# Moving the second layer's modulation sums from the first mixer into the second and third

## The reference

```python
def second_block(x, c, ada_w, ada_b, ln_g, ln_b, ...):
    cond = jax.nn.silu(c)
    for l in range(DEPTH_2):                                   # 2 layers
        mod = (cond @ ada_w[l] + ada_b[l])[:, None, :]         # 1024 -> 6 * 1024
        sh_m, sc_m, g_m, sh_f, sc_f, g_f = jnp.split(mod, 6, axis=-1)
        h = x * (1.0 + sc_m) + sh_m
        y = even_mixer(h, ...) if l % 2 == 0 else spatial_gating_mixer(h, ...)
        x = layer_norm_2(ALPHA * x + (1.0 + g_m) * y, ln_g[l, 0], ln_b[l, 0])
        h = x * (1.0 + sc_f) + sh_f
        y = swiglu(h, ...) if l % 2 == 0 else moe_swiglu(h, ...)
        x = layer_norm_2(ALPHA * x + (1.0 + g_f) * y, ln_g[l, 1], ln_b[l, 1])
    return x
```

## Time and profile before

| what | value |
|---|---|
| three executions, median (lowest to highest) | 2375.59 us (2375.39 to 2376.65) |
| the profiled execution, its own time | 2377.7 us |
| its span in the trace | 2375.9 us |
| TensorE matmul busy | 2269.4 us (96%) |
| VectorE busy | 1608.5 us (68%) |
| ScalarE busy | 1297.5 us (55%) |
| read from HBM | 635.29 MB |
| TensorE clock granted, mean over the span | 0.982 |

### The profile page before, as it was taken

The page is one execution under the profiler, slowest core; times in us unless marked ns, Lnnn a source line. Parts: engine busy times, 40 slices in busy tenths (PEclk is TensorE's granted clock), DMA queues, the critical chain, the costliest instruction groups (busy, mean ns, idle before and its releaser), DMA issues.

```text
span 2375.9 us, 25462 instructions
## 1 busy us (share of the span) xinstructions
PE 2269.4 (96%) x10290; PEld 1857.8 (78%) x10290; DVE 1608.5 (68%) x1897; ACT 1297.5 (55%) x1562; POOL 0.4 (0%) x6
## 2 busy tenths in 40 slices
PE   8999999998999979799989899999999999999997
PEld 7668877887888866578848788888888888888886
DVE  0266233546889863345423698989898998989895
ACT  1245113105677743334320587877777787878784
POOL 0000000000000000000000000000000000000000
PEclk9999999997999999999999799999999999999999
DMA  8465455745998862045440498999999898989892
GB/s 345 185 255 213 178 212 233 274 195 223 359 356 327 325 266 107 1 177 213 161 176 1 194 391 335 365 347 354 349 353 377 325 372 327 374 328 376 326 374 96
DMA packets 51217, 638.14 MB, mean 269 GB/s; under 512 B 8737, under 2 KB 10638, under 8 KB 12302
## 3 DMA queue, kind: packets, MB, share of 16 engines
q1 hardware_dynamic: 48526, 630.33, 69.1%
q10 hardware_dynamic: 2560, 6.03, 0.7%
HBM read 635.29 MB, written 1.05 MB: 268 GB/s over the span
## 4 chain that ended last, share of the span: by engine, by line
PE 91%; DVE 4%; ACT 2%; DMA 2%; issue 1%; SPq 0%; DVEq 0%; ACTq 0%
PE psum L1697 56%; PE psum L1487 19%; PE psum L1479 5%; PE psum L1707 2%; PE psum L1581 2%; PE psum L1720 2%; PE psum L1787 2%; DMA ring<-w_in 1%; DMA ring<-w_branch_in 1%; DVE stage_lo L1338 1%; PE psum L1592 0%; ACT arena L546 0%; DMA ring<-w_in_in 0%; DVE arena L559 0%; PE psum L1509 0%
## 5 line engine op out<-in xcount | busy, mean ns | idle before, releaser
L1338 DVE TENSOR_TENSOR stage_lo<-ring,stage_hi 128x1024 fp32r<-128x1024 f32 (+1 forms) x934 | 1109.6, 1218 | 107.4 <-ACT stage_hi L926 82.7
L926 ACT ACTIVATE stage_hi<-ring 128x1024 fp32r<-128x1024 f32 (+1 forms) x934 | 965.3, 1056 | 279.0 <-PE psum L1697 247.9
L1697 PE MATMUL psum<-stage_hi,x_hi 128*128 128x512 f32 (+1 forms) x1344 | 529.1, 394 | 14.2 <-DVE x_lo L1320 11.5
L1697 PE MATMUL psum<-stage_hi,x_lo 128*128 128x512 f32 (+1 forms) x1344 | 522.3, 389 | 0.0
L1697 PE MATMUL psum<-stage_lo,x_hi 128*128 128x512 f32 (+1 forms) x1344 | 521.1, 388 | 0.0
L1697 PEld LDWEIGHTS psum<-stage_hi,x_hi 128*128 128x128 f32 x1344 | 253.2, 188 | 64.1 <-issue 11.9
L1697 PEld LDWEIGHTS psum<-stage_hi,x_lo 128*128 128x128 f32 x1344 | 253.0, 188 | 53.0
L1697 PEld LDWEIGHTS psum<-stage_lo,x_hi 128*128 128x128 f32 x1344 | 253.5, 189 | 49.3
L1697 PE MATMUL psum<-stage_hi,h_hi 128*128 128x512 f32 x664 | 259.9, 391 | 4.8 <-DVE h_lo L1377 4.8
L1697 PE MATMUL psum<-stage_lo,h_hi 128*128 128x512 f32 x664 | 258.6, 389 | 0.0
L1487 PE MATMUL psum<-arena,ring 128*128 128x256 f32 x1024 | 227.0, 382 | 6.3 <-DVE arena L1285 4.3
(11 more groups left out here) (210 smaller groups left out, 1764.5 us busy)
## 6 DMA issues: line engine op xcount, KB each, us to landing
ring<-moe_w_gate_in SPq DMA_DIRECT2D x56, 2048.0 KB, 9.5
ring<-moe_w_up_in SPq DMA_DIRECT2D x56, 2048.0 KB, 9.6
ring<-moe_w_down_in SPq DMA_DIRECT2D x56, 2048.0 KB, 9.4
ring<-w_in SPq DMA_DIRECT2D x48, 2048.0 KB, 9.6
ring<-ada_w_in SPq DMA_DIRECT2D x15, 2048.0 KB, 7.9
ring<-w_in_in SPq DMA_DIRECT2D x14, 2048.0 KB, 10.8
mixer_tiles<-ada_w_in SPq DMA_DIRECT2D x9, 2048.0 KB, 7.9
mixer_tiles<-w_in_in SPq DMA_DIRECT2D x6, 2048.0 KB, 12.8
```

Of the source, the lines that this page charges most:

```text
L926: act.activation(chunk_view(stage_hi, f, side, p, c), chunk_source(f, side, p, c), ACT.Copy)\
L1338: dve.tensor_tensor(chunk_view(stage_lo, f, side, p, c), chunk_source(f, side, p, c), chunk_view(stage_hi, f, side, p, c).bitcast(F32), AL ...
L1697: ins = pe.matmul(dst, a, b, start=start, stop=stop)
```

## The change

The `ada` steps of layer 1 leave mixer 1. Six of them go to mixer 2 and six to mixer 3. Those of layer 0 all stay in mixer 1: four move to the start (two after `da_k`, two after `da_v`), four stay in the retention heads, four stand in the memory heads; none is left in the attention heads, in `gate2` or in `branch2`. Each `ada` step now loads and sums its own panel, so the panel planner's special cases go, and so does the first sum ahead of the walk. The bias and `1 + mod` are now made in three pieces: columns 0 to 47 at the end of layer 0, 48 to 71 at the sixth panel of layer 1 (in mixer 2), 72 to 95 at the twelfth (in mixer 3). The condition vector stays in SBUF meanwhile.

```diff
@@ mixer1_steps
-    s += [("gemm", "da_q", i) for i in range(4)] + [("gemm", "da_k", i) for i in range(4)]
+    s += [("gemm", "da_q", i) for i in range(4)]
+    for i in range(4):
+        s += [("gemm", "da_k", i)] + ([("ada", 0, i // 2)] if i % 2 else [])
     s += [("vec", 0, 0), ("vec", 1, 0)]
     s += [("turn_mem", i, 0) for i in range(4)]
-    s += [("gemm", "da_v", i) for i in range(4)]
+    for i in range(4):
+        s += [("gemm", "da_v", i)] + ([("ada", 0, 2 + i // 2)] if i % 2 else [])
...
-        s += [fill.pop(0), ("da_turn", h, 0)] + ([("ada", 0, h)] if h < DA_H - 1 else []) + [("da_out", h, 0)]
+        s += [fill.pop(0), ("da_turn", h, 0)] + [("da_out", h, 0)]
...
-    s += [("gemm", "branch0", i) for i in range(4)] + [("ada", 0, DA_H - 1)]
+    s += [("gemm", "branch0", i) for i in range(4)]
...
-        s += [("ret_out", h, 0), fill.pop(0), ("ada", 0, DA_H + h), ("ret_mean", h, 0)] + fill[:1] + [("ret_var", h, 0)]
+        s += [("ret_out", h, 0), fill.pop(0), ("ada", 0, 4 + h), ("ret_mean", h, 0)] + fill[:1] + [("ret_var", h, 0)]
...
-        s += [("mem_score", h, 0), fill.pop(0), ("mem_turn", h, 0), fill.pop(0), ("mem_out", h, 0), ("ada", 1, h)]
+        s += [("mem_score", h, 0), fill.pop(0), ("mem_turn", h, 0), fill.pop(0), ("mem_out", h, 0), ("ada", 0, 8 + h)]
     for n in ("gate2", "branch2"):
         for i in range(4):
-            s += [("gemm", n, i)] + [("ada", 1, MEM_H + (4 if n == "branch2" else 0) + i)]
+            s += [("gemm", n, i)]
@@ mixer2_steps
-    s += [("gemm", "ev_q", i) for i in range(2)]
-    s += [("ev_k", 0, 0), ("ev_v", 0, 0), ("gqa_score", 0, 0), ("gqa_score", 1, 0)]
+    s += [q for i in range(2) for q in (("gemm", "ev_q", i), ("ada", 1, i))]
+    s += [("ev_k", 0, 0), ("ada", 1, 2), ("ev_v", 0, 0), ("gqa_score", 0, 0), ("gqa_score", 1, 0)]
...
-        s += [("gqa_out", h, 0)]
+        s += [("gqa_out", h, 0)] + ([("ada", 1, 3 + h // 2)] if h in (1, 3, 5) else [])
@@ mixer3_steps
-    s += [("gemm", "od_v", i) for i in range(4)] + [("gemm", "od_u", i) for i in range(4)]
+    for n, name in enumerate(("od_v", "od_u")):
+        for i in range(4):
+            s += [("gemm", name, i)] + ([("ada", 1, 6 + 3 * n + i)] if i < 3 else [])
@@ plan_loads
-            elif s == ("da_score", 0, 0) or s[0] == "ada" and s != ("ada", 1, 11):
-
-                m = 0 if s[0] == "da_score" else 12 * s[1] + s[2] + 1
-                key = ("ada", m // 12, m % 12)
-                src, free = w["ada_w_2"][m // 12, m % 12], (ada_summed, m + 1)
+            elif s[0] == "ada":
+
+                src, free = w["ada_w_2"][s[1], s[2]], (ada_summed, 12 * s[1] + s[2] + 1)
@@ ScalarE, before each feed
-            act.wait_ge(ada_summed, 24)
+            act.wait_ge(ada_summed, (12, 18, 24)[n])
@@ VectorE, walk
-                    n = 12 * a + i + 1
-                    if n < 24:
-                        sum_modulation(n)
-                    else:
-                        evacuated(("vec", 1, 0))
+                    if (a, i) == (0, 0):
+                        dve.wait_ge(cond_set, 1)
+                    sum_modulation(12 * a + i)
+                    if (a, i) in ((0, 11), (1, 5), (1, 11)):
...
-        dve.wait_ge(cond_set, 1)
-        sum_modulation(0)
```

More of the change, by code:

```diff
@@ L1287, in modulate @@
                                    .then_inc(modulated, 1)
-                    if a == 1:
-                        dve.wait_ge(modp1_set, 1)
+                    if a in (1, 3, 4):
+                        dve.wait_ge(modp1_set, (1, 0, 2, 3)[a - 1])
                     layer_norm_vector(dve, settle, a, src, done[s], job_bank(s), bank_through(s),
```

10 lines of the change are left out of this document (7 added, 3 removed).

## The result

The changed kernel took 2386.95 us (median of six, 2384.72 to 2388.15) against 2375.49 us (2372.89 to 2376.83) for the kernel before, run beside it. The ratio is 1.0045 with a 95% interval from 1.0034 to 1.0056: slower by 11.5 us, between 8.1 and 13.3. The forecast was slower by 8.2 us, 2383.8 us, in a range up to 2389.0. So the sign and the main mechanism were right, and the size was 3.3 us short.

What follows compares the result with a forecast made beforehand. The prediction took TensorE's work plus its waits to bound the kernel, with VectorE setting the pace jointly in mixer 2's attention. Terms -0.6 + 0.2 + 7.6 + 1.0 = +8.2 us on the 2375.6 us median gave 2383.8 us, range 2379.0 to 2389.0.

Steps and rivals of the forecast that it cites:

- branch2: Mixer 1: TensorE's 0.60 us wait for a `branch2` panel goes, the one before `w_o` stays; -0.6 us, bounds -2.2 and 0.
- da_v: Start of mixer 1: the second `da_v` panel, loaded after a sum, may land late; +0.2 us, bounds 0 and 1.7.
- Sums 1 to 3: Mixer 2 before the first scores: three sums of 14.0 us are hidden by TensorE's `ev_q` and `ev_k`; 0 us.
- ev_p: Mixer 2: its panel, now loaded later, lands in 7.7 us, wanted after 8.0; 0 us, bounds 0 and 1.4.
- Sums 4 and 5: Mixer 2's attention: sums behind head 3's and head 5's softmax delay later softmaxes and `ev_o`; +7.6 us, bounds 4.9 and 11.6.
- The clock: Mixer 2's attention: TensorE's clock likely falls after about 5 us of waiting before head 5's output; +1.0 us, bounds 0 and 3.2.
- The signs: New trace: `ev_o` starts 75 to 77 us after `ev_q`, `ev_p` waits at most 0.3 us, `od_u` and gating as before.
- The sums and loads of feed 1 and mixer 3: Feed 1's first panel and mixer 3's six sums fit into idle time: 0 us, up to 2 if `od_u` panels land late.
- (a): Rival: mixer 2's sums fit into slack, only 4.9 us paid and no clock lost; +4.5 us, 2380.1 us; chance 0.12.
- (b): Rival: sums cause mixer 1's attention waits, so 8.7 us go, down to 2366.9 us; chance 0.03 faster, 0.02 within 0.2%.
- (c): Rival: loads issued together share the queue evenly, so `ev_p` and `da_v` wait; +23.1 us, 2398.7 us; chance 0.04.

Runs made afterwards that it cites:

- e1: The changed kernel with its three sums in mixer 2's attention moved behind VectorE's work on `ev_o`'s jobs 0, 1 and 2: 2377.91 us, ratio 1.0004.
- e3: The changed kernel with only the sum behind head 5's softmax left in mixer 2's attention, the other two behind `ev_o`'s jobs 0 and 1: 2385.40 us, ratio 1.0044.
- e4b: The changed kernel with 4 and 5 unread matmuls filling TensorE's waits ahead of the outputs of heads 3 and 5: 2388.56 us, ratio 1.0053.
- e5: The changed kernel with one attention sum left, behind head 1's softmax, its load ahead of `ev_p`'s; other two behind `ev_o`'s jobs 0 and 1: 2386.96 us, ratio 1.0043.
- e6: The changed kernel with the sums behind head 3's and head 5's softmax made twice: 2398.39 us, ratio 1.0092.
- e2: The changed kernel with only the sum behind head 3's softmax left in mixer 2's attention, the other two behind `ev_o`'s jobs 0 and 1: 2385.63 us, ratio 1.0045.
- e4: The changed kernel with 8 and 10 unread matmuls ahead of the outputs of heads 3 and 5, longer than the waits: 2393.14 us, ratio 1.0074.
- e5b: As e5, but with the load of `ev_p`'s panel put first again, ahead of the sum's panel: 2376.93 us, ratio 0.9999.
- e7: The changed kernel with mixer 2's six sums back in mixer 1, beside `gate2` and `branch2`; start and mixer 3 kept: 2377.33 us, ratio 0.9997.
- e9: e1 with unread matmuls in TensorE's waits around norms and routers, and ahead of feed 1, the first gating and the last transposes: 2369.07 us, ratio 0.9965.

## Why the prediction was right, and where it was not

- **`branch2`, -0.6.** Right. The wait of the earlier trace rows is gone, the one before `w_o` is 1.62 us instead of 1.56.
- **`da_v`, +0.2.** Right. Its second panel is used at 86.48 instead of 84.24, of which 2.0 us stood there before the first sum (73.84 instead of 71.85). Those 2.0 us lie in the very first job, which ends at 22.39 instead of 20.40 although its panel came no later. They are no cost of the change: with the same start of the kernel this job ends at 21.8 to 22.4 in e1, e3, e4b, e5 and e6 and at 20.2 to 20.4 in e2, e4, e5b and e7.
- **Sums 1 to 3, +0.** Right. They end at 908.2, and VectorE then waits 5.89 us for the first scores.
- **`ev_p`, +0.** Right. Issued at 905.99, the panel landed 7.7 us later with two loads behind it, and the first matmul at 913.98 has no wait. The rule of the Trainium skill that I cited ("DMA: Bandwidth & Descriptors", queues, rings and completion order) agrees, and e5 shows its other side: there the panel had one load ahead of it and came 12.4 us after its issue, the load ahead of it 7.9 us after its own.
- **Sums 4 and 5, +7.6.** Right: 7.7 us in e4b, where the clock does not mix in. The steps were not all exact. Softmax 6 starts at 954.59, 9.3 us late against the first score and not 8.3, because half clock slowed head 4's transposes (in e4b it is 8.1). And the first wait, which I had put at 2 us or somewhat more, is 3.85 us before head 3's output: I had seen ScalarE's copy queued behind exponentials only at head 5.
- **The clock, +1.0, bounds 0 to 3.2.** This is the term that failed by size. I counted only a fall behind the 5 us wait and let part of it pass in waiting. The 3.85 us wait brings one too. In the attention the clock cost 2.6 us. With it the sum would have been 7.2 + 2.6 = 9.8. The Trainium skill's penalty ("TensorE: Matmul & The Clock Gate", Terms) overstates this part: 23 us at a mean of 0.70 are 13.8 us at half clock, an estimate of 6.9 us by its formula, and the runs show 2.6; much of the slow time fell into waits. `ev_q` took 16.67 us instead of 15.95, but that is no cost of the sums: it took 16.46 in e1 and 16.28 in e7, which run at the time of the kernel before, and 15.80 in e2.
- **What the sum left out: half clock in mixer 3, 1.8 us.** The norm behind `od_o` computes its sum of squares with 16 matmul instructions. They run in part at half clock in the changed kernel, behind a wait of 2.07 us:

```profile
1328.08 5.37 PE L1585 MATMUL psum<-arena 128*128 128x256 f32 x16 [2.07 <-ACT arena L541]
```

In the kernel before they run at full clock behind nearly the same wait:

```profile
1316.36 3.69 PE L1581 MATMUL psum<-arena 128*128 128x256 f32 x16 [2.00 <-ACT arena L538]
```

The sums of mixer 3 are not the reason, for e1, e5, e5b and e7 have them too and are longer by 0.1 us only. But every kernel with a sum behind head 3's or head 5's softmax has the loss: 1.8 us in the change, e2, e4, e4b and e6, and 1.1 in e3 (there in `od_v`). So it may well belong to their cost, 370 us behind them; 9.8 + 1.8 = 11.6 would account for the 11.5 measured. With one profile of each kernel that is not shown, and nor is how the one would bring about the other.
- **The signs.** `ev_o` comes 968.35 - 889.29 = 79.1 us after `ev_q`, and not the 75 to 77 forecast: that is the clock again. `ev_p`, `od_u` and the gating came as written. The upper end of the range is 2388.9 by its own terms, not 2389.0.
- **The sums and loads of feed 1 and mixer 3, +0.** Right. ScalarE's first read in feed 1 waits 0.62 us for VectorE as before. In mixer 3 VectorE keeps 9.56 us of idleness before its normalisation and 3.36 before the first gating, where I had worked out 3. e7 confirms that the six sums there cost nothing.
- **Rivals.** (a), slack, fell with e6: there is none in these gaps. (b) fell with the 134.49 us of the first stretch. (c) fell with the 7.7 us landing. In e5 the panel did come late, but behind a load ahead of it, which is not the even sharing that (c) supposed.

What stays open: why each gap alone costs nearly as much as both. From the norm ahead of mixer 2 to the one behind mixer 3, the change is 13.0 us longer than the kernel before, e2 11.5 and e3 11.0, of which the chain is 7.7, 4.7 and 4.3. The rows show where the half clock lies, into `ev_o` and in the norm behind feed 1 in e2 and e3 and not in the change, but not what sets its end. And the last stages differ by several microseconds between executions with the same instructions there (feed 2 and the last norm took between 1044.5 and 1052.3 us), so a single profile doesn't close the sum to better than some 3 us.

## What to carry to other kernels

An engine that is half idle in a stage may still have no slack at all in the place where work is put: look at the gap itself, and ask which queue stands behind it (here ScalarE's copy behind exponentials behind a sum). Work of 4.7 us was free ahead of head 2's softmax, where VectorE waits for `ev_p` anyway, and between the jobs of `ev_o`, and cost 9 us between two later softmaxes. And where a step also places its load, moving one moves both: check what it then goes ahead of in the queue. A filling belongs where the engine itself waits: one step too early it delays that step, and the wait stays (e9).
